# Three DRAM copies behind the last expert weights, and ScalarE as the one that asks for the routed sums

## What is computed

```
h   = RMSNorm(x) * (1 + scale1(c)) + shift1(c)
qa, ka, va, fa, qb, kb, vb = split(h @ w_in)
oa  = forgetting attention (prompt; samples over a paged cache, with suffix sums of the forget gates)
ob  = dilated sliding-window attention (prompt; samples over window buffers)
x   = x + gate1(c) * (concat(norm(oa), norm(ob)) @ w_o)
h2  = RMSNorm(x) * (1 + scale2(c)) + shift2(c)
x   = x + gate2(c) * (routed(h2) + shared(h2))      # 64 experts of width 256, top 8 of each token
return x, the new K, V and forget rows, ..., ek[:, 1:], ev[:, 1:]
```

## Time and profile before

| | |
|---|---|
| time, median of 3 runs | 1340.4 us (1339.69 to 1340.46) |
| span of the profiled execution | 1340.1 us |
| TensorE busy | 1180.0 us, 88% |
| mean granted clock of TensorE | 0.944 |
| share of 16 DMA engines, queues q1, q0, q10 | 67.6%, 19.1%, 6.5% |
| bytes moved, mean | 457.71 MB, 342 GB/s |

### The profile page before, as it was taken

The page is one execution under the profiler, slowest core; times in us unless marked ns, Lnnn a source line. Parts: engine busy times, 40 slices in busy tenths (PEclk is TensorE's granted clock), DMA queues, the critical chain, the costliest instruction groups (busy, mean ns, idle before and its releaser), DMA issues.

```text
span 1340.1 us, 17713 instructions
## 1 busy us (share of the span) xinstructions
PE 1180.0 (88%) x5832; PEld 612.8 (46%) x5832; DVE 485.1 (36%) x1389; ACT 273.6 (20%) x612; POOL 239.8 (18%) x281
## 2 busy tenths in 40 slices
PE   3999999956777888999999999999899989899891
PEld 1687774324343335445445444444344434344440
DVE  2356457034453332335623332223232322232226
ACT  2222342122333134022111111111111111111110
POOL 0200000022323130000012222222121222222110
PEclk9999999968888797999999999999899989999996
DMA  9979999999999997999799999999999899989844
GB/s 369 422 288 348 339 367 322 334 283 346 367 382 339 335 393 309 360 314 360 268 369 336 355 380 380 389 389 358 382 356 390 297 396 349 365 329 382 306 164 144
DMA packets 93534, 457.71 MB, mean 342 GB/s; under 512 B 15848, under 2 KB 17416, under 8 KB 76672
## 3 DMA queue, kind: packets, MB, share of 16 engines
q1 hardware_dynamic: 59552, 347.80, 67.6%
q0 software_dynamic: 28384, 80.43, 19.1%
q10 hardware_dynamic: 5504, 28.32, 6.5%
HBM read 435.13 MB, written 106.77 MB: 404 GB/s over the span
## 4 chain that ended last, share of the span: by engine, by line
PE 63%; DMA 17%; SPq 7%; DVE 7%; issue 4%; ACT 1%; ACTq 1%; POOLq 0%; DVEq 0%
PE banks L750 20%; PE banks L774 10%; DMA reg_w<-in_w_down 10%; PE banks L1742 7%; PE banks L583 4%; PE banks L1732 3%; PE banks L737 2%; SPq L1576 2%; PE banks L645 2%; DVE reg_s L1998 2%; SPq L1577 2%; PE banks L1909 2%; SPq L1395 1%; DMA reg_q<-in_cache_k 1%; PE banks L1867 1%
## 5 line engine op out<-in xcount | busy, mean ns | idle before, releaser
L750 PE MATMUL banks<-reg_q,reg_w 128*128 128x512 f32 (+1 forms) x528 | 203.7, 619 | 20.4 <-issue 18.4
L750 PEld LDWEIGHTS banks<-reg_q,reg_w 128*128 128x128 f32 (+1 forms) x528 | 78.9, 173 | 139.8 <-issue 139.6
L774 PE MATMUL banks<-reg_q,reg_w 128*128 128x512 f32 (+1 forms) x324 | 134.4, 608 | 1.1 <-DMA reg_w<-in_w_down 0.6
L1152 DVE SCALAR_TENSOR_TENSOR reg_w<-banks,small,reg_w 128x256 f32<-128x256 f32 x50 | 24.2, 484 | 306.2 <-ACT reg_w L1345 306.2
L1498 POOL DMA_INDIRECT reg_w<-h_rows,gidx x50 | 52.3, 1046 | 401.9 <-DVE gidx L1113 352.7
L1502 POOL DMA_INDIRECT routed_sum<-reg_w,sidx x64 | 97.5, 1523 | 147.7 <-issue 75.4
L1345 ACT ACTIVATE reg_w<-banks 128x256 f32<-128x256 f32 x50 | 19.2, 384 | 433.9 <-PE banks L750 433.9
L1742 PE MATMUL banks<-hT,reg_q 128*128 128x260 f32 x384 | 88.2, 389 | 3.9 <-DVE spare L1964 2.3
L1195 DVE COPY reg_w<-banks 128x512 f32<-128x512 f32 x50 | 34.6, 692 | 128.4 <-PE banks L774 128.4
L1742 PEld LDWEIGHTS banks<-hT,reg_q 128*128 128x128 f32 x384 | 73.7, 193 | 15.4 <-issue 4.3
L750 PE MATMUL banks<-hT,reg_w 128*128 128x512 f32 (+1 forms) x176 | 78.1, 597 | 0.0
(11 more groups left out here) (375 smaller groups left out, 1573.9 us busy)
## 6 DMA issues: line engine op xcount, KB each, us to landing
reg_q<-in_w_gate_up SPq DMA_DIRECT2D x33, 2048.0 KB, 36.1
reg_q<-in_w_down SPq DMA_DIRECT2D x33, 1024.0 KB, 35.6
out_win_k_s<-in_win_k SPq DMA_DIRECT2D x8, 4094.0 KB
out_win_v_s<-in_win_v ACTq DMA_DIRECT2D x6, 4094.0 KB
reg_w<-in_w_ada SPq DMA_DIRECT2D x11, 2048.0 KB, 13.1
hT<-in_w_gate_up SPq DMA_DIRECT2D x11, 2048.0 KB, 35.6
spare<-in_w_gate_up SPq DMA_DIRECT2D x10, 2048.0 KB, 37.8
reg_s<-in_w_gate_up SPq DMA_DIRECT2D x10, 2048.0 KB, 44.4
```

The source lines that it names most:

```text
L750: last = mm(pb[j % 2][of, :], lhsT=xT[:, j % 2, k, of], rhs=wgu[LOAD[p] % NBUF][:, k, :], start=(k == 0), stop=(k == KC - 1))
L774: last = mm(pb[6 + hh][of, :], lhsT=aT[:, j % 2, c, of], rhs=down_w(LOAD[p] % NBUF, c, hh), start=(c == 0), stop=(c == 1))
```

## The change

`COPY_AT` loses its last three places, so SP issues seven copies in the front instead of ten. ScalarE's six copies stay at their places, with numbers 7 to 12 instead of 10 to 15. The last three copies, 13 to 15, are issued by SP behind its last load of expert weights. The loads of both sums go from SP to ScalarE: those of sum 1 behind the result of unit 46 (`j == NU - LATE`), those of sum 0 behind ScalarE's test for more tokens.

```diff
--- before.py
+++ after.py
@@ -131,9 +131,11 @@
 NTAKEN = NW + 2
 
 NLATE = 6
-
-COPY_AT = sorted([AT["qk", n] for n in range(4, 16, 2)] + [AT["v", 0], AT["v", 2], AT["vs", 0], AT["v", QB + 2]])
-assert len(COPY_AT) == 2 * NS - NLATE
+NTAIL = 3
+NEARLY = 2 * NS - NLATE - NTAIL
+
+COPY_AT = sorted([AT["qk", n] for n in range(4, 16, 2)] + [AT["v", 0]])
+assert len(COPY_AT) == NEARLY
 
 
 NB = 36
@@ -1269,7 +1271,7 @@
                 A(junk[0:n_, :], x[0:n_, t, :], ACT.Square, accum_out=ss[0:n_, t:t + 1]).then_inc(squares, 1)
                 act.wait_ge(squares, SQ0 + 2 * QB + t + 1)
                 A(ss[0:n_, t:t + 1], ss[0:n_, t:t + 1], ACT.Sqrt, scale=1.0 / D, bias=EPS).then_inc(roots, 1)
-                for n in range(2 * NS - NLATE - (-t * NLATE // TT), 2 * NS - NLATE - (-(t + 1) * NLATE // TT)):
+                for n in range(NEARLY - (-t * NLATE // TT), NEARLY - (-(t + 1) * NLATE // TT)):
                     copy_window(act, n, win_out)
 
             def copy_h2(t):
@@ -1359,6 +1361,12 @@
                 for n in range(2 if j >= 2 else 0):
                     act.wait_ge(*landed_sums(n, j - 2))
                 C(y[:, u, 0:512], pb[6][:, :]).then_inc(yA_set, 1)
+                if j == NU - LATE:
+                    act.wait_ge(y_ready, 2 * (NU - LATE) + 2)
+                    act.wait_ge(scattered[1], 16 * (ZEROS + added(1, NE)))
+                    for t in range(TT):
+                        n_ = rows_of[t]
+                        act.dma_start(rows[t][1][0:n_, :], rsum[1][t * P:t * P + n_, :]).then_inc(rows_in[t], 16)
             act.wait_ge(m_over, 1)
             more = act.value_load(over[0:1, 0:1], min_val=0, max_val=OVER)
             with act.If(more > 0):
@@ -1369,6 +1377,11 @@
                         A(sg[:, 0, :], pb[0][:, 0:F], ACT.Silu).then_inc(sg_set, 1)
                         act.wait_ge(a_turned, j + (NU + 1))
                         C(aT[:, 0, :, :].rearrange("p a b -> p (a b)"), pb[4][:, 0:2 * P]).then_inc(aT_set, 1)
+            act.wait_ge(y_step, 2 * TT)
+            act.wait_ge(routed_done, 1)
+            for t in range(TT):
+                n_ = rows_of[t]
+                act.dma_start(rows[t][0][0:n_, :], rsum[0][t * P:t * P + n_, :]).then_inc(rows_in[t], 16)
 
         def sync_after(sp):
             sp.wait_ge(ring_used, len(ITEMS))
@@ -1454,11 +1467,8 @@
                     sp.wait_ge(y_ready, 2 * j + 2)
                 for n in after(j):
                     dn_of(n)
-            sp.wait_ge(y_ready, 2 * (NU - LATE) + 2)
-            sp.wait_ge(scattered[1], 16 * (ZEROS + added(1, NE)))
-            for t in range(TT):
-                n_ = rows_of[t]
-                sp.dma_start(rows[t][1][0:n_, :], rsum[1][t * P:t * P + n_, :]).then_inc(rows_in[t], 16)
+            for n in range(2 * NS - NTAIL, 2 * NS):
+                copy_window(sp, n, win_out)
             sp.wait_ge(route_set, 1)
             more = sp.value_load(over[0:1, 0:1], min_val=0, max_val=OVER)
             with sp.If(more > 0):
@@ -1472,11 +1482,6 @@
                         sp.dma_start(wdn[0].rearrange("p a b -> p (a b)"), I["w_down"][ds(expert, 1), :, :].rearrange("a p n -> (a p) n")
                                      ).then_inc(m_in, 16)
 
-            sp.wait_ge(y_step, 2 * TT)
-            sp.wait_ge(routed_done, 1)
-            for t in range(TT):
-                n_ = rows_of[t]
-                sp.dma_start(rows[t][0][0:n_, :], rsum[0][t * P:t * P + n_, :]).then_inc(rows_in[t], 16)
             for t in range(TT):
                 n_ = rows_of[t]
                 sp.wait_ge(y_step, 2 * TT + 2 * t + 2)
```

## The result

The changed kernel takes 1348.64 us, the median of 20 runs (1344.28 to 1351.53); the kernel before took 1341.65 us in 20 runs beside them. The ratio is 1.0047, 95% interval [1.0034, 1.0059]: slower by 6.3 us. All ratios here leave disturbed runs out; there is one, at 1443.63 us, of v2_tail2. The profiled execution has a span of 1349.8 us, 9.7 more than that of before. It is the slowest of the 20 runs (1351.53 us), so the pair of traces shows a larger difference than the medians do.

A forecast was written before the change was run, and what follows sets the result against it. TensorE, 88% busy, was taken as the bound, so copies matter only where a late transfer idles it. Front -12.1, scatters +10.8, test +0.8, sum 0 loads +5 give +4.5: 1344.5 us, own range 1341 to 1348, wider range 1333 to 1351.

The forecast's parts named there:

- The front: Up to the last weights: three copies fewer in SP's queue make everything 12.1 us earlier, bounds 11 and 15.
- The steps to TensorE: At attention: ScalarE's load issue no longer hangs, so sample fold and attention matmuls come some 11.3 us earlier, near 271.
- the step to SP: After attention starts: SP's small stores move by 11.3 us and its page loads then carry the lead, giving another 0.8.
- The jam's end: In the front: the full DMA queues clear near 246 us instead of 283, three copies being 37.5 us of all engines.
- The rival in which the jam lasts: Front: weights alone keep queues full to 262, gain 0 to 6 us; part of a rival with chance 0.07, 1349 to 1355.
- The scatters: Tail: beside the copies the last scatters land after 11.0 us each at a pitch of 11.85, costing 10.8 us.
- The reasoning about half of the engines: Behind the last weights: about 8 DMA engines stay full until 1292.5 and 8 are free, so copies start late there.
- The test: Before sum 0: ScalarE's test for more than one round waits for VectorE's late signal, costing 0.8 us, bounds 0.3 and 3.
- The loads of sum 0: At the kernel's end: they share engines with 15.8 us of copies left, costing 5 us, the middle of 0 and 10.6.
- the rival in which the copies outlast the adds: Tail: copies on the slow engines last to 1355.2 with stores of y behind them; 1350 us, chance 0.11.
- The rule against the row: Sum 0's loads: engines serve queues whole packets in turn, so loads end with the copies, +10.6 for +5, 1350; 6.4-to-1 packet ratio cited.
- Hidden copies: Tail rival: copies fill idle engines, scatters land after 6 to 8 us, tail +1 to +8; about 1333 us, chance 0.24.

The follow-up runs named there:

- v2_tail2: The changed kernel with two copies behind the last expert weights instead of three, and eight in front; ratio to the kernel before 1.0019.
- e1: The kernel before with seven copies in front instead of ten, the three made nowhere, SP still loading the sums; ratio 0.9924 to the kernel before.
- v1: The changed kernel with one copy behind the last expert weights instead of three, and nine in front; ratio to the kernel before 0.9964.
- e4: The changed kernel with ScalarE's wait for VectorE's late signal moved into the branch not entered; ratio to the kernel before 1.003.
- e3: The changed kernel with no copies behind the weights and ten in front, so only the sums' loads moved to ScalarE; ratio to the kernel before 1.0006.
- w2: The kernel before with only the copy at 252.97 us issued at 65 instead, all sixteen copies made; 1332.57 us, ratio 0.9922 to the kernel before.

## Why the prediction was right, and where not

- **The sign, and the sum.** +4.5 us forecast, +6.3 [4.6, 7.9] measured; 1344.5 against 1348.64. The structure held: a gain in front, eaten by scatters and not by TensorE. The time lies 0.6 us over the forecast's own range of 1341 to 1348 and within the wider one. That the sum came so near is in part luck: against the trace the scatters were 2.1 us too cheap and the loads of sum 0 3.3 us too dear, and the front was 1.9 us too good against the time of e1.
- **The front, forecast 12.1.** Without any tail it is 10.2 by time [6.8, 13.6]. The steps to TensorE were right (11.1 us at attention). Mis-sized was the step to SP: I wrote that its small stores move by the same 11.3, but they stand behind page loads that wait for TensorE's last projection and are issued until 273.1, and the page loads behind them moved by 8.55. I also let everything up to the last weights move by 12; in the pair of traces the scatter of unit 46 moves by 6.0. The 6.7 at the projection and this 6.0 must not be read too finely: from SP's copy at 205 to the projection's first run of 32 matmuls it is 326.3 us in the trace of before and 322.2 and 322.6 in two more with the copy at 253, and 314.8 to 319.4 in the eleven without it; the changed kernel's is the longest of these. So executions of fronts that hold a copy at 253 differ by 4 us among themselves, and those that do not by 4.6.
- **The jam's end, forecast 246.** The engines empty near 227. Taking 37.5 from 283 was too simple a model; nothing hung on it, since one copy less is enough for the loads of the suffix sums to go in 2.9 us (v1). The rival in which the jam lasts has fallen.
- **The scatters, forecast 10.8.** 12.9 in the trace: landings of 12.95, 10.39 and 10.33 us at a pitch of 13.3, 13.8 and 11.2, where I took 11.0 and 11.85. The reasoning about half of the engines fits everything seen (share 1.00 to 1300, then about half while copies last, and in v1 and v2 6 us again for the last scatters), though no view shows the engines one by one.
- **The test, forecast 0.8:** 1.1 in the trace, and gone in e4.
- **The loads of sum 0, forecast 5:** 1.7. I had 15.8 us of copies left on the full engines at the request at 1330.21; the last 5 packets of them go between 1332.5 and 1334. Two sizes were off: from 1300 to 1320 a copy's packet took 36.1% of 320 us over 385, 0.300 us, where I had 0.391, and a scatter's 144 packets at 12.8% of 320 over 273 took 21.6 engine-us, 2.7 for each of eight engines, where I had 4.7. With both, and from the landing of the last weights in this trace (1256.19 + 33.8 = 1290.0), it is 1290.0 + 28.8 + 5.6 + 3 x 2.7 = 1332.5, near what is seen. So the rival in which the copies outlast the adds has fallen. And I left out a cost: behind its late test ScalarE's loads are 1.2 us slower with no copy in the system (e3).
- **The rule against the row.** The rule of the Trainium skill that I weighed (DMA: Bandwidth & Descriptors, Queues, rings and completion order) was priced at 10.6 here. That price needed 15.8 us of copies to be left, and from 1331 to 1332.5 q1 moved only 15 packets beside the 51 of q10, so no run here tests it. I also called the ratio of 6.4 to 1 an agreement; the rule names no ratio between two queues, so that row neither bears it out nor refuses it.
- **Hidden copies (0.24).** Half right: from 1260 to 1300 they do fill idle engines, and with a single copy the last two scatters are nearly undisturbed (v1). But the two scatters ahead of them are slow even then, and for three copies it does not hold at all.

## What to carry to other kernels

Look for the one bulk transfer that is in flight when small loads are asked for which others wait for, and move that one: here the whole gain in front was in one copy, and a place 188 us earlier took it for free. A mean DMA share of one half behind the last weights is not room for bulk work if what follows is a chain of transfers that wait for each other; look at what a transfer takes there, not at the share. Price such places by adding copies one at a time, since they differ in kind: at the output projection six copies were free and the seventh cost 10.6 us, a step; behind the last weights the first already cost 1.5 to 3.4 us of scatters and each further one 4 to 6 more, a slope.

## What was not expected of the hardware

An accumulating scatter of the same 0.26 MB in 144 packets lands after 6.0 us alone and after 10.3 to 13 us beside copies in another queue, though from 1300 on the engines are only half busy in the mean (0.41 to 0.58). The last weights do much the same to it: before, the scatter at 1286.35, while they were landing, took 9.6 us. And an issuing engine that hangs 15 to 16 us on a DRAM copy (SP at 205 or 219 us in every kernel here with eight to ten copies in front) is harmless as long as the engine that computes has work: w2 keeps that hang and loses nothing.
